# Tile 5 of the key selection: from the bit search on ScalarE to rounds of eight on VectorE

## What is computed

```
index_score = einsum('bths,bth->bts', relu(idx_logits), wi_b)   # every query t against every key s
index_score = where(causal, index_score, neg)
_, sel = lax.top_k(index_score, n_sel)          # n_sel = 256
s = einsum('bthc,btkc->bthk', ql_b, c[sel])     # attention over the kept keys only
p = softmax(where(valid, s, neg))
```

## Time and profile before

| | before |
|---|---|
| median of 3 runs | 2403.91 us |
| the profiled execution | 2408.83 us |
| its span (first to last instruction) | 2407.0 us |
| PE busy | 2334.2 us (97%) |
| DVE busy | 1314.7 us (55%) |
| ACT busy | 943.4 us (39%) |
| POOL busy | 409.5 us (17%) |

### The profile page before, as it was taken

The page is one execution under the profiler, slowest core; times in us unless marked ns, Lnnn a source line. Parts: engine busy times, 40 slices in busy tenths (PEclk is TensorE's granted clock), DMA queues, the critical chain, the costliest instruction groups (busy, mean ns, idle before and its releaser), DMA issues.

```text
span 2407.0 us, 32363 instructions
## 1 busy us (share of the span) xinstructions
PE 2334.2 (97%) x12937; PEld 1777.2 (74%) x12937; DVE 1314.7 (55%) x2232; ACT 943.4 (39%) x1689; POOL 409.5 (17%) x614
## 2 busy tenths in 40 slices
PE   7999999999999999999999999999989999999998
PEld 7887888888777898788878887778755554745554
DVE  5567777242214365577763322336678856447644
ACT  6345556131113243355551311141354548822231
POOL 0034220000000001333100000000148952401011
PEclk9999999999999999999999999999999999999999
DMA  6010001222113210100021222224101011200000
GB/s 220 31 53 1 1 1 37 63 53 53 37 43 140 72 71 31 53 1 2 1 71 27 53 53 53 62 105 150 36 1 45 1 45 45 101 22 27 27 18 35
DMA packets 106645, 116.92 MB, mean 49 GB/s; under 512 B 20832, under 2 KB 78912, under 8 KB 106496
## 3 DMA queue, kind: packets, MB, share of 16 engines
q1 hardware_dynamic: 106208, 113.81, 15.2%
q10 hardware_dynamic: 288, 1.05, 0.1%
HBM read 96.82 MB, written 16.84 MB: 47 GB/s over the span
## 4 chain that ended last, share of the span: by engine, by line
PE 90%; DVE 5%; ACT 2%; issue 1%; POOL 1%; DMA 0%; SPq 0%; DVEq 0%; ACTq 0%
PE PS L732 8%; PE PS L792 7%; PE PS L795 7%; PE PS L798 7%; PE PS L564 7%; PE PS L756 5%; PE PS L950 5%; PE PS L1204 4%; PE PS L845 2%; PE PS L1173 2%; PE PS L1151 2%; PE PS L838 2%; PE PS L841 2%; PE PS L842 2%; PE PS L617 1%; PE PS L619 1%
## 5 line engine op out<-in xcount | busy, mean ns | idle before, releaser
L795 PE MATMUL PS<-hLo,R2bR 128*128 128x512 f32 x768 | 299.0, 389 | 0.0
L792 PE MATMUL PS<-hHi,R2bR 128*128 128x512 f32 x752 | 293.3, 390 | 0.0
L798 PE MATMUL PS<-hHi,R2bR 128*128 128x512 f32 x752 | 292.7, 389 | 0.0
L2303 DVE TENSOR_TENSOR R2bR<-W,R2bR 128x1024 fp32r<-128x1024 f32 x48 | 57.5, 1222 | 267.3 <-ACT R2bR L1575 267.3
L1642 ACT ACTIVATE R3a<-PS,pT 128x512 f32<-128x512 f32 x64 | 42.3, 688 | 403.6 <-PE PS L798 403.5
L1591 ACT ACTIVATE R2b<-PS,negm 128x1024 f32<-128x1024 f32 x128 | 142.6, 1114 | 62.3 <-DVE negm L2282 62.2
L950 PE MATMUL PS<-hT,W 128*128 128x512 f32 x384 | 166.0, 593 | 0.7 <-ACT R L1742 0.7
L795 PEld LDWEIGHTS PS<-hLo,R2bR 128*128 128x128 f32 x768 | 144.3, 188 | 29.5
L2282 DVE TENSOR_REDUCE negm<-PS 128x1 f32<-128x1024 f32 x128 | 156.5, 1222 | 17.0 <-PE PS L732 16.3
L792 PEld LDWEIGHTS PS<-hHi,R2bR 128*128 128x128 f32 x752 | 141.4, 188 | 30.1 <-issue 0.5
L798 PEld LDWEIGHTS PS<-hHi,R2bR 128*128 128x128 f32 x752 | 141.3, 188 | 29.6
(11 more groups left out here) (495 smaller groups left out, 5314.3 us busy)
## 6 DMA issues: line engine op xcount, KB each, us to landing
W<-in_w_in SPq DMA_DIRECT2D x10, 2048.0 KB, 8.3
W<-in_w_in SPq DMA_DIRECT2D x33, 512.0 KB, 4.3
W<-in_w_out SPq DMA_DIRECT2D x6, 2048.0 KB, 7.8
xres<-R SPq DMA_DIRECT2D x2, 4096.0 KB, 15.3
R<-xres SPq DMA_DIRECT2D x2, 4096.0 KB, 18.4
W<-in_w_in SPq DMA_DIRECT2D x4, 1024.0 KB, 6.5
R3a<-rsums SPq DMA_DIRECT2D x16, 256.0 KB, 5.5
W<-in_w_attn_proj SPq DMA_DIRECT2D x16, 256.0 KB, 5.8
```

The costliest lines, as they stand in the source:

```text
L792: mm = pe.matmul(o, wHi[c % 2][:, k, :], hi, start=(k == 0), stop=False)
L795: mm = pe.matmul(o, wHi[c % 2][:, k, :], hLo[:, k, ns], start=False, stop=False)
L798: mm = pe.matmul(o, wLo[c % 2][:, k, :], hi, start=False, stop=(k == 7))
L2303: dve.tensor_tensor(wLo[c % 2], w, wHi[c % 2].bitcast(F32), ALU.subtract).then_inc(s_wlo, 1)
```

## The change

Tile 5 leaves the bit search. `SEARCHED` becomes `(7, 6)`, so each of the 32 steps counts two tiles on ScalarE and has two L2543 on VectorE. `take_eight`, unchanged, now also reaches tile 5: round k works on tile 3 + k // 32, so rounds 64 to 95 are tile 5's 32 rounds. Rounds 64 to 82 (19) stand with the steps: one more behind step 25, three behind each of the steps 26 to 31. Rounds 83 to 95 (13) stand in the attention loop at the even units 8 to 32; the last of them is followed by the operation that makes the mask. `choose(2)` goes.

```diff
-SEARCHED = (7, 6, 5)
+SEARCHED = (7, 6)
 SEARCH_STEPS = 32
+EARLY_EIGHTS = 83
...
                 act.wait_ge(s2_bound, i + 1)
-                if 3 * i + c > 0:
-                    act.wait_ge(s2_sign, 3 * i + c)
+                if 2 * i + c > 0:
+                    act.wait_ge(s2_sign, 2 * i + c)
...
-                    for c in range(3):
+                    for c in range(len(SEARCHED)):
                         count_signs(i, c)
...
                 for c, t in enumerate(SEARCHED):
-                    dve.wait_ge(s2_sign, 3 * i + c + 1)
+                    dve.wait_ge(s2_sign, 2 * i + c + 1)
...
             for i in range(11, SEARCH_STEPS):
                 next_bounds(i)
-                take_eights(34 + 2 * (i - 11), 2 * (i < 26))
+                take_eights(34 + 2 * (i - 11) + max(i - 25, 0), 2 + (i >= 25))
...
-                if 16 <= u < 32 and u % 2 == 0:
-                    choose(2, (u - 16) // 2)
+                if 8 <= u <= 32 and u % 2 == 0:
+                    take_eights(EARLY_EIGHTS + (u - 8) // 2, 1)
                 if 32 <= u < 48:
                     choose(1 - (u - 32) // 8, u % 8)
```

More of the change, by code:

```diff
@@ L306, in build @@
         m8 = ssc[:, 0:8]
-        signs_sum, minus = negm[:, 48:51], negm[:, 51:54]
-        drop_bit, minus_bits = negm[:, 54:57].bitcast(mybir.dt.int32), minus.bitcast(mybir.dt.int32)
+        signs_sum, minus = negm[:, 48:50], negm[:, 51:53]
+        drop_bit, minus_bits = negm[:, 54:56].bitcast(mybir.dt.int32), minus.bitcast(mybir.dt.int32)
         U = r0[:, 0:4096].rearrange("p (j c) -> p j c", j=CL)
@@ L1889, in _ @@
                         if (tp, hp) == (6, 0):
-                            act.wait_ge(s2_chosen, 3)
+                            act.wait_ge(s2_chosen, 2)
                         act.activation(PT2[hp // 4][:, 4:4 + n, (hp % 4) * P:(hp % 4 + 1) * P],
```

## The result

The changed kernel takes 2417.65 us (median of 4 runs, 2416.94 to 2419.85) against 2404.91 us of the kernel before (4 runs, 2403.84 to 2406.54) beside it. The ratio is 1.0047, 95% interval 1.0031 to 1.0063. It is slower, and by about what was forecast (2416.0). A second series gave 1.0039 (1.0027 to 1.0052).

What follows compares the result with a forecast made beforehand. TensorE, busy 97% of the span, was taken as the bound; other engines count only where it waits. +5.8 (Part 3 with Part 1) + 1.0 (clock) + 5.8 (Part 4) - 0.5 (Part 2) = +12.1 on 2403.91: 2416, range 2406 to 2422.

Steps and rivals of the forecast that it cites:

- Part 1: Search steps: 32 counts fewer on ScalarE; the gate near 1978 comes sooner, gain 1.1 us, the other 31 counts nothing.
- Part 2: Search steps: one L2543 fewer shortens the threshold update, which may start ahead of GpSimd's operation; gain 0.5, between 0 and 1.8.
- "faster" rival: Relief ahead of TensorE's 4.11 us wait for GpSimd, clock perhaps not dropping: at most 4.7 us gained, 2399; chance 0.08.
- Part 3: End of the GLU: 19 rounds of 2.05 us with the steps delay the first scores; +5.8 with Part 1's gain inside.
- the signs that I had set myself: Part 3 fails if first scores start before 2103; TensorE's wait in L1136 under 3 us also shows the forecast wrong.
- The wait of some 6 us: End of the GLU, L1136: TensorE's banks are full and it stands some 6 us for VectorE's first evacuation.
- The 1.5 us for meetings with GpSimd: GLU window: each of six moved updates has half a chance to wait 0.65 on average; 0 to 4, taken 1.5.
- The clock term: Start of attention: the 6 us hole may hold TensorE's lower clock longer; 0 to 4 us, taken 1.
- Part 4: Attention: 13 rounds at even units 8 to 32, `choose(2)` out; +5.8 us, between 3 and 8.
- unit 33 against unit 31: Attention, sign for the round at unit 32: unit 33's maximum later by 2.6 than unit 31's.
- The rival of thin tiles at the lower clock: Tiles 0 and 1 keep the clock down until `out_half`: +3 over the 1 taken, 2419, or 2421; chance 0.19.
- the rival of rounds that hide: VectorE idles a third of the attention, so rounds hide better than counted: +8.3 us, 2412; chance 0.18.

Runs made afterwards that it cites:

- second series: The changed kernel timed again, unaltered, against runs of the kernel before: 2417.44 us (5 runs), ratio 1.0039.
- the two kernels with three small operations: Kernel before without `choose(2)`: 2402.99 us, 0.9982; changed kernel without rounds for 768 keys, with a third small operation per step: 2402.71 us, 0.9981.
- the 19 rounds: Changed kernel with only the search's 19 rounds for 768 keys, the attention's 13 left out: 2410.20 us, ratio 1.0009 to before.

## Why the prediction was right, and where it was not

Its sum was +12.1, against +10.1 and +10.4 in the traces and +9.7 and +12.7 by medians. The +12.7 is against four runs of before with a median of 2404.91; the longer series of before have 2407.7 to 2408.4, so the distance is known to about 3 us. By terms:

- **Part 1** (1.1 for the third count): right. 1.2 between the two kernels with three small operations that differ by the count.
- **Part 2** (0.5, at most 1.8): the mechanism was right, the size too small. All the updates in question slipped ahead of GpSimd's operation (0.16 or 0.17 us each), worth 1.5. What I left out of both parts, and put only into the "faster" rival, is the clock: 2.3 us more of half clock behind the two waits are in the traces of before than in those of the changed kernel, 1.6 of them behind the second. Together A gave 5.0 for my 1.6. This is the largest error, 3.4 us.
- **Part 3**: the row of MAX8 is as worked out.

```profile
L2534 DVE MAX8 ssc<-R2a 128x8 f32<-128x768 f32 x32 | 30.6, 955 | 0.4
L2535 DVE MATCH_REPLACE8 R2a<-ssc,R2a 128x768 f32<-128x768 f32 x32 | 30.2, 943 | 0.0
```

  VectorE, from the changed kernel's timeline, has no idle time ahead of its first evacuation:

```profile
2093.97 0.96 DVE L2534 MAX8 ssc<-R2a 128x8 f32<-128x768 f32 x1
2094.97 0.09 DVE L2535 MATCH_VALUE_LOAD R2a<-ssc,R2a 128x8 f32 x1
2095.05 0.94 DVE L2535 MATCH_REPLACE8 R2a<-ssc,R2a 128x768 f32<-128x768 f32 x1
2096.02 4.31 DVE L2630 TENSOR_SCALAR R<-PS 128x512 f32<-128x512 f32 x7
```

  That is 2096.0 for a predicted 2101.6, and first scores at 2101.35 for 2106.9. Both are 5.6 early since the GLU starts at 2040.3, 5.7 sooner than the 2046.0 that my part 1 implied. By the signs that I had set myself (first scores before 2103, a wait in L1136 under 3 us) part 3 would have failed; the first was an absolute time, which the earlier GLU moved. Measured from the GLU's start B is 61.1, and predicted were 60.9, and a step with three rounds took 6.48 us (2062.85 to 2069.33) for my 6.5. The wait of some 6 us came in two, 2.96 and 2.83, of which I had only the second. The first is ScalarE's, and it costs nothing beyond the second, as said above. It is ended by an evacuation that stands behind the counts, and these wait for thresholds that VectorE issues behind three rounds:

```profile
2083.53 1.15 ACT L1723 ACTIVATE signs<-R2b,negm 128x1024 int8<-128x1024 f32 x1 [2.85 <-DVE negm L2551]
...
2084.87 1.04 ACT L1723 ACTIVATE signs<-R2a,negm 128x896 int8<-128x896 f32 x1
...
2087.05 0.59 ACT L1861 ACTIVATE u_mid<-PS 128x512 f32<-128x512 f32 x1
```

  The 1.5 us for meetings with GpSimd were too much (two of the seven updates met it, 0.64 and 0.49 us long), the size of a round was right.
- **The clock term** (1, of 0 to 4): 0 or 1.7 in B (3.0 in one trace with the 19 rounds), then up to 3.2 in C (1.2 at tile 4 whenever the round at unit 32 is there, 2.0 at tile 2 in three traces of five). The changed kernel has 3.2 of it in its first trace and 2.9 in its second. I had looked for it in tile 0 and 1, where it makes little: 8.47 and 9.07 us to unit 8, where before takes 8.86.
- **Part 4** (5.8): +7.9 between the columns of before and changed, +6.6 in the second trace. By units, changed minus before at 11, 17, 21, 25, 33, 36: 0.7, 1.5, 3.2, 3.9, 6.7, 7.9. My running sum was 1.4, 2.3, 2.6, 2.9, 5.8, 5.8. Unit 32 with its 2.6 is as worked out (6.7 at unit 33 against 4.05 at unit 32), though the sign that I had named, unit 33 against unit 31, shows 1.4 only: unit 31 is 5.3 later than before, and 1.3 of that is gained back by unit 32. Units 8 and 10 cost 1.05 (from unit 8 to 11) of my 1.4; unit 11 is only 0.7 late since unit 8 came 0.4 sooner. What is over is the clock, at 17 to 25 and at 33 to 36. The working was of differences, and it hides that the rounds cost 11.4 over nothing and `choose(2)` some 3 (3.5 between these columns, 2.8 in C when it was taken out by itself).

So the verdict was right because the mechanisms of both losses were. That the number came within 2 us is in part luck: 3.4 too little relief in A stood against some 2 too little clock in B and C, and the rounds in the attention were 0.4 to 1 cheaper than worked out once the clock is taken off.

Of the rivals, the one with relief at the two waits ("faster") described a real gain: the update slipped ahead and the wait fell to 3.05. Its clock came differently: the sixteen products behind that wait still took 3.20 and 3.59 us (1.95 at full clock), and more was saved behind the second wait. It was wrong in that the rounds are not cheap where the change puts them; put elsewhere, they let the gain through. The rival of thin tiles at the lower clock had its condition in the second trace (0.52 of full from 2104 to 2108), but there only 0.6 us more than in the first up to unit 8. The share by which VectorE idles in the attention was set too low in the rival of rounds that hide: in the first 105 us before it is busy 56.7, so 46% are idle and not a third, and the rounds still did not hide.

## What to carry to other kernels

Two traces of kernels that start the same are compared from the last common point on, stretch by stretch, and not by their spans. Here the stretches repeat within 0.3 us, save for falls of the clock, while the part ahead varies by 5 to 6. Then, work for an engine that is idle 45% of the time is free only where the idle time is: the same 32 rounds cost 18.5 us over none at all behind the last steps and beside the heads (9.7 over before against 8.8 under it), and 1 to 3 us, within the spread, where VectorE idled. When an engine waits twice in a row, the sum of the waits is no price: here the second wait's end was fixed by VectorE, and the first, with the slow products behind it, cost nothing. A new or a vanishing wait of TensorE gets a second term for the clock, with a chance: here 0 to 3 us behind waits of 1.2 to 4.5 us.

## What the runs showed of the hardware

- The clock behind one and the same wait falls in some executions and not in others: after 1.79 and 1.82 us of idle time at the second gate it was at half (0.65 us for four small products) or at full (0.39); after the second wait in B it fell behind 2.97 and 3.06 us (5.40 us for 14 products) and 4.52 us (6.77), and behind 2.83 it did not (3.70); behind the first wait there, 2.96 to 2.99 us each time, it fell in three traces (6.03 to 6.25 us for 18 products) and held in one (4.56). After 2.8 us at tile 4 it fell in four traces of four, after 1.5 us at tile 2 in three of five.
- A small operation of 0.06 us more on VectorE decides whether the one behind it takes 0.17 or 1.23 us, as it starts just ahead of or just behind an operation of GpSimd. From the changed kernel's timelines of VectorE and GpSimd:

```profile
1853.59 0.17 DVE L2549 TENSOR_SCALAR negm<-negm 128x2 int32<-128x2 int32 x1
```

```profile
1853.60 5.07 POOL L2819 TENSOR_TENSOR R3b<-R3a,R3b 128x508 f32<-128x508 f32 x4
```

  In before it is the other way round, 1855.50 and 1855.44. With the third small operation added it is so again, 1854.13 and 1854.09, and the update takes 1.23 us.
